# Two attention layers on one core: rotary columns of four heads per weight group, keys in four banks, filter steps moved

## The reference, cut to what matters

```python
h = rmsnorm(x, g_mix[l]);  p = h @ w_in[l]
c_q = rmsnorm(p[..., :384], g_q[l])
q = (c_q @ w_uq[l]).reshape(b, s, 8, 64 + 32)        # 8 heads, 64 plain columns + 32 rotary columns each
q_rope = apply_rope(q[..., 64:], cos, sin)           # t1*cos - t2*sin, t2*cos + t1*sin
c_kv = rmsnorm(p[..., 384:640], g_kv[l])
kv = (c_kv @ w_ukv[l]).reshape(b, s, 8, 64 + 64)     # keys, values
k_rope = apply_rope(p[..., 640:672], cos, sin)       # one for all heads
y_attn = attention(q_nope, q_rope, k_nope, k_rope, v)
a, gt = split(p[..., 672:], 2);  u = a * sigmoid(gt)
u = dwconv(u, w_dw_conv[l], b_dw_conv[l])            # 31 taps over 512 channels
u = silu(layernorm(u, g_conv_ln[l], b_conv_ln[l]))
x = x + concat([y_attn, u]) @ w_o[l]                 # then the feed-forward part
```

## Time and profile before

| | |
|---|---|
| median of three runs | 1910.74 us |
| the profiled execution: its time | 1910.56 us |
| its span, first to last instruction | 1908.8 us |
| TensorE busy, mean granted clock | 96% of the span, 0.982 |
| VectorE, ScalarE busy | 70%, 52% |
| chain that ended last | TensorE 76%, VectorE 11%, no wait shown 6%, ScalarE 6% |

### The profile page before, as it was taken

How to read it: one execution, slowest core, us unless ns; L and a number is a source line. 1 busy time by engine, 2 the same in 40 slices (tenths; PEclk the granted TensorE clock), 3 DMA queues, 4 the chain that set the end, 5 groups by cost and what they waited for, 6 DMA issues and landing times.

```text
span 1908.8 us, 27050 instructions
## 1 busy us (share of the span) xinstructions
PE 1824.7 (96%) x8939; PEld 1451.0 (76%) x8939; DVE 1331.8 (70%) x1873; ACT 986.3 (52%) x1556; POOL 191.7 (10%) x135
## 2 busy tenths in 40 slices
PE   6989999999999998999999999997998999999998
PEld 5765778888888875678888888886655678888887
DVE  6979777777655888967777755695676477777544
ACT  5478654444433478764444433674655554444322
POOL 0100120000133200020000033200012300000111
PEclk9999999999999998999999999998999999999999
DMA  5230233333233330023333233434000223332332
GB/s 168 71 77 1 66 90 98 91 97 96 82 94 111 92 83 12 29 83 100 98 99 99 74 97 94 110 94 133 1 2 1 89 67 98 99 99 82 88 98 75
DMA packets 294697, 154.47 MB, mean 81 GB/s; under 512 B 29621, under 2 KB 292695, under 8 KB 294615
## 3 DMA queue, kind: packets, MB, share of 16 engines
q1 hardware_dynamic: 294196, 153.26, 28.0%
q10 hardware_dynamic: 419, 0.17, 0.0%
HBM read 151.31 MB, written 2.10 MB: 80 GB/s over the span
## 4 chain that ended last, share of the span: by engine, by line
PE 76%; DVE 11%; issue 6%; ACT 6%; DMA 0%; DVEq 0%; SPq 0%; ACTq 0%
PE bank L548 23%; PE bank L550 23%; PE bank L549 23%; DVE cacc L1674 4%; DVE w_lo L1537 2%; PE bank L921 1%; PE bank L961 1%; PE bank L940 1%; DVE nmax L1757 1%; ACT w_hi L1120 1%; DVE pr L2002 1%; PE bank L700 1%; DVE nmax L1986 1%; PE bank L1036 0%; DMA x_in<-in_x 0%
## 5 line engine op out<-in xcount | busy, mean ns | idle before, releaser
L1120 ACT ACTIVATE w_hi<-raw 128x1024 fp32r<-128x1024 f32 (+2 forms) x321 | 333.5, 1041 | 507.2 <-PE bank L550 502.4
L1537 DVE TENSOR_TENSOR w_lo<-raw,w_hi 128x1024 fp32r<-128x1024 f32 (+2 forms) x321 | 401.3, 1251 | 260.6 <-ACT w_hi L1120 259.9
L548 PE MATMUL bank<-h_hi,w_hi 128*128 128x512 f32 x1448 | 570.3, 394 | 10.8 <-DVE w_lo L1537 10.7
L549 PE MATMUL bank<-h_lo,w_hi 128*128 128x512 f32 x1448 | 564.9, 390 | 0.0
L550 PE MATMUL bank<-h_hi,w_lo 128*128 128x512 f32 x1448 | 564.8, 390 | 0.0
L548 PEld LDWEIGHTS bank<-h_hi,w_hi 128*128 128x128 f32 x1448 | 272.7, 188 | 74.8 <-issue 11.7
L549 PEld LDWEIGHTS bank<-h_lo,w_hi 128*128 128x128 f32 x1448 | 272.7, 188 | 58.2 <-issue 2.2
L550 PEld LDWEIGHTS bank<-h_hi,w_lo 128*128 128x128 f32 x1448 | 272.7, 188 | 57.1
L548 PE MATMUL bank<-a_hi,w_hi 128*128 128x512 f32 x528 | 206.1, 390 | 0.0
L550 PE MATMUL bank<-a_hi,w_lo 128*128 128x512 f32 x528 | 205.5, 389 | 0.0
L549 PE MATMUL bank<-a_lo,w_hi 128*128 128x512 f32 x528 | 205.4, 389 | 0.0
(11 more groups left out here) (314 smaller groups left out, 2217.5 us busy)
## 6 DMA issues: line engine op xcount, KB each, us to landing
raw<-in_w_up SPq DMA_DIRECT2D x132, 512.0 KB, 3.7
raw<-in_w_in SPq DMA_DIRECT2D x39, 512.0 KB, 3.9
raw<-in_w_down SPq DMA_DIRECT2D x48, 384.0 KB, 3.1
raw<-in_w_down SPq DMA_DIRECT2D x48, 320.0 KB, 2.9
raw<-in_w_o SPq DMA_DIRECT2D x16, 512.0 KB, 3.5
raw<-in_cmp_w SPq DMA_DIRECT2D x8, 512.0 KB, 4.0
raw<-in_w_out SPq DMA_DIRECT2D x8, 512.0 KB, 4.7
x_in<-in_x SPq DMA_DIRECT2D x4, 512.0 KB, 7.5
```

Of the source, the lines that this page charges most:

```text
L548: mm(o, wh, mh, start=start, stop=False)
L549: mm(o, wh, ml, start=False, stop=False)
L1120: last = A_(dst(w_hi), src(raw), ACT.Copy)
L1537: last = v.tensor_tensor(dst(w_lo), src(raw), dst(w_hi).bitcast(f32), ALU.subtract)
```

## The change

In the first two layers:

- Query slabs 0 and 3 are the wide ones (`UQ_N`); slab 3 carries the rotary columns of heads 4 to 7, into bank 6, and TensorE's wait for the rotary keys goes with it. The four small DMAs of the rotary columns move from slab 2 to slab 3.
- The tables lie in `sq` and `ssq2`, tensors of their own, and are copied at input slabs 2 to 5, two copies each.
- The keys use banks 4, 2, 0, 3, each once; their waits are for query copies (`qn_done`), and values and scores wait for the key copies instead.
- VectorE: all four cosine products of the second group stand together, behind the value slab's low part; 18 filter steps are issued around the query and key slabs where there were 10, and 3 at each step of attention where there were 4.

```diff
-        tabs = at("tabs", [P, 2, SEQ], 0)
...
-        UQ_B, K_B, V_B = ((0, 1), (2,), (3, 6), (5,)), (4, 2), (0, 1, 3, 6)
+        UQ_B, K_B, V_B = ((0, 1), (2,), (3,), (5, 6)), (4, 2, 0, 3), (0, 1, 3, 6)
+        UQ_N = (2, 1, 1, 2)
...
-                    if j == 2:
+                    if j == 3:
                         pe.wait_ge(kr_done.sem, kr_done.at(L, 1))
...
-                    if i == 1:
-                        pe.wait_ge(qn_done.sem, qn_done.at(L, 4))
-                    elif i > 1:
-                        pe.wait_ge(k_done.sem, k_done.at(L, 2 * (i - 1)))
+                    if i >= 1:
+                        pe.wait_ge(qn_done.sem, qn_done.at(L, (0, 4, 4, 6)[i]))
...
-                        pe.wait_ge(k_done.sem, k_done.at(L, H - 2))
+                        pe.wait_ge(k_done.sem, k_done.at(L, 2))
...
+                    if t % 2 == 0:
+                        pe.wait_ge(k_done.sem, k_done.at(L, 6 + t))
...
-                    if i >= 12:
-                        for q in (2 * i - 24, 2 * i - 23):
-                            for z in range(2):
-                                A_(tabs[q * ROPE:(q + 1) * ROPE, z, :], trig[z * ROPE:(z + 1) * ROPE, :], ACT.Copy).then_inc(tab_done.sem, 1)
+                    if 2 <= i < 6:
+                        q = slice((i - 2) * ROPE, (i - 1) * ROPE)
+                        A_(sq[q, :], trig[0:ROPE, :], ACT.Copy).then_inc(tab_done.sem, 1)
+                        A_(ssq2[q, :], trig[ROPE:2 * ROPE, :], ACT.Copy).then_inc(tab_done.sem, 1)
...
-                dve.wait_ge(slab_used.sem, g * RAW + (S_UQ + 3))
+                split(g, S_UQ + 2 + SPL)
+                conv(2)
+                dve.wait_ge(slab_used.sem, g * RAW + (S_UQ + 4))
                 sine_part(1)
-                split(g, S_UQ + 2 + SPL)
-                cosine_part(1, 0, 2)
                 split(g, S_UQ + 3 + SPL)
-                cosine_part(1, 2, 4)
+                cosine_part(1, 0, 4)
+                conv(8)
                 conv(6)
-                conv(3)
                 split(g, S_UKV + SPL)
-                conv(1)
+                conv(2)
...
-                    conv(4)
+                    conv(3)
```

More of the change, by code:

```diff
@@ L436, in split_aps @@
             if S_UQ <= n0 < S_UKV:
-                used = lambda w: w[:, n0 % w.shape[1], 0:KQ * P * (2 - (n0 - S_UQ) % 2)]
+                used = lambda w: w[:, n0 % w.shape[1], 0:KQ * P * UQ_N[n0 - S_UQ]]
                 return [(used, used)]
@@ L483, in _ @@
                 for j in range(H // 2):
-                    n = P * (2 - j % 2)
+                    n = P * UQ_N[j]
                     to = slot(S_UQ + j, KQ, n)
@@ L492, in _ @@
                             sp.dma_start(dst, src).then_inc(uq_ready[j], 16)
-                    if j % 2 == 0:
+                    if UQ_N[j] == 2:
                         for q in range(4):
-                            sp.dma_start(to[:, :, P + q * ROPE:P + (q + 1) * ROPE], of[:, :, 2 * j + q, NOPE:HQ]).then_inc(uq_ready[j], 16)
+                            sp.dma_start(to[:, :, P + q * ROPE:P + (q + 1) * ROPE], of[:, :, j // 2 * 4 + q, NOPE:HQ]).then_inc(uq_ready[j], 16)
                 for z in range(2):
@@ L660, in _ @@
                         pe.wait_ge(u_done.sem, u_done.at(L, KC))
-                    w = parts(S_UQ + j, KQ, P * (2 - j % 2))
-                    for z in range(2 - j % 2):
+                    w = parts(S_UQ + j, KQ, P * UQ_N[j])
+                    for z in range(UQ_N[j]):
                         for k in range(KQ):
@@ L673, in _ @@
                 for i in range(H // 2):
-                    if i == 1:
-                        pe.wait_ge(qn_done.sem, qn_done.at(L, 4))
-                    elif i > 1:
-                        pe.wait_ge(k_done.sem, k_done.at(L, 2 * (i - 1)))
+                    if i >= 1:
+                        pe.wait_ge(qn_done.sem, qn_done.at(L, (0, 4, 4, 6)[i]))
                     for k in range(KKV):
-                        last = mm3(bank[K_B[i % 2]][:, :], [z[:, k, i * P:(i + 1) * P] for z in w],
+                        last = mm3(bank[K_B[i]][:, :], [z[:, k, i * P:(i + 1) * P] for z in w],
                                    (c_hi[:, KQ + k, :], c_lo[:, KQ + k, :]), k == 0, k == KKV - 1)
@@ L1113, in split @@
                     j = n0 - S_UQ
-                    act.wait_ge(uq_ready[j], (L + 1) * 16 * (1 + 4 * (1 - j % 2)))
+                    act.wait_ge(uq_ready[j], (L + 1) * 16 * (1 + 4 * (UQ_N[j] - 1)))
                 if not isinstance(g, int) and S_UKV <= n0 < S_O:
@@ L1262, in _ @@
                     for e in range(2):
-                        A_(kT[0:NOPE, 2 * i + e, :], bank[K_B[i % 2]][e * NOPE:(e + 1) * NOPE, :],
+                        A_(kT[0:NOPE, 2 * i + e, :], bank[K_B[i]][e * NOPE:(e + 1) * NOPE, :],
                            ACT.Copy).then_inc(k_done.sem, 1)
@@ L1719, in sine_part @@
                 def sine_part(z):
-                    v.scalar_tensor_tensor(qs[:, z, :], bank[UQ_B[2 * z][1]][:, :], SCALE1, tabs[:, 1, :], ALU.mult, ALU.mult)\
+                    v.scalar_tensor_tensor(qs[:, z, :], bank[UQ_B[3 * z][1]][:, :], SCALE1, ssq2[:, :], ALU.mult, ALU.mult)\
                         .then_inc(qs_done.sem, 1)
@@ L1725, in cosine_part @@
                         r = slice(q * ROPE, (q + 1) * ROPE)
-                        v.scalar_tensor_tensor(qT[64:96, 4 * z + q, :], bank[UQ_B[2 * z][1]][r, :], SCALE1, tabs[r, 0, :],
+                        v.scalar_tensor_tensor(qT[64:96, 4 * z + q, :], bank[UQ_B[3 * z][1]][r, :], SCALE1, sq[r, :],
                                                ALU.mult, ALU.mult).then_inc(qr_done.sem, 1)
```

## The result

| | before | after |
|---|---|---|
| median | 1909.65 us (1907.61 to 1913.0, 5 runs) | 1918.92 us (1917.78 to 1919.41, 5 runs) |
| profiled execution: time, span | 1910.56, 1908.8 | 1919.41, 1917.6 |
| mean granted clock | 0.982 | 0.980 |

The change is slower by 9.3 us: ratio 1.0045, 95% interval 1.003 to 1.0059. The prediction was 1909.7 us, range 1904.0 to 1915.5; the time lies outside, on the side of rival B.

A forecast was written before the change was run, and what follows sets the result against it. TensorE, busy 96% of the span, was taken to bound the kernel, with VectorE arriving almost together at the sums. A gain of 0.5 us per layer, 1.0 in all, from the median of 1910.74 gave 1909.7 us, range 1904.0 to 1915.5.

The forecast's parts named there:

- rival B: Ahead of the sums: low clock behind TensorE's new wait, 1.7 to 3.3 us per layer, time 1914.7; chance 0.23.
- The tables cost nothing: Table copies moved to input slabs 2 to 5: cost 0 there, gain 0.5 us on ScalarE.
- front of slabs: Ahead of the keys: table and wide-slab moves together start the keys at 120.9 us and not at 121.40.
- C: Filter's end: VectorE isn't late, so unit 15's 3.3 us count in full, 6.6 in all, 1904.1; chance 0.25.
- D: Whole change does nothing, since unit 0's scores still need ScalarE's queue: 1910.7 us; chance 0.06.
- forecast A: Front's gain ends in TensorE's wait for the filter: 1908 to 1911.5 us; chance 0.46.
- Attention: Unit 6 to unit 15: TensorE leads, 1.6 us gained, plus 1.7 ahead of that; unit 15's scores 3.3 earlier.
- The end of the filter: Unit 15's maxima to the sums: VectorE has 14 steps left, TensorE waits 3.3 us; gain 0.5 us per layer.
- I took 0.3 us for it: Filter steps behind unit 1's maxima: extra cost of running beside POOL's first sum, taken as 0.3 us.
- The bound of 0.9: Filter steps beside POOL's sum: nearest row allows 0.9 us extra; in full, gain 0 per layer and 1910.7.

The follow-up runs named there:

- before again: The kernel before, unedited, profiled once more beside the unedited change: 1908.23 us.
- two shifted kernels: The kernel before with 17, and in a second kernel 8, overwritten matmuls added at the start of the third layer: 1913.21 and 1908.92 us.
- The filled wait: The changed kernel with 16 overwritten matmuls in TensorE's wait ahead of the sums: 1912.49 us, ratio 1.0017 to before.
- second batch: Both kernels, unedited, measured and profiled once more: before 1908.23 us, change 1919.12 us, ratio 1.0057.

## Why the prediction was wrong

**What held.** The place of each event in layer 1 held. The profiled execution of the change comes to that layer 0.73 us earlier than before's (first query slab at 105.03 against 105.76), so 0.73 is added to its times here. The key wait is gone. TensorE waits 2.06 us ahead of unit 0's scores (2 predicted) and 3.03 ahead of unit 2's (3.5). The first maximum is at 139.4 (139.5). From unit 6 on attention goes at TensorE's pace, 3.81 us a step, and unit 15's scores are at 194.7 (194.1). The low part of `yq` comes 1.41 us late (1.5), and TensorE waits 3.83 ahead of the sums (3.3). The tables cost nothing, and the front of slabs gained 0.45. Rivals C and D fell, and the forecast A too.

**The step that failed first is the base of the sum**, in "Attention": "Ahead of that the wait at 157.66 and the low clock behind it go or shrink: 1.7." The wait behaves as said, but that low clock was an event of one execution. Three others of the same code in these layers (before again, and the two shifted kernels) do without it, and their layers take 124.6 to 125.4 us where the rows had 127.4. The prediction set beside the median (1910.74) only that execution's total (1910.56), and the total hid it: that execution was long in the layers and short in the third layer (654.8, against 656.9 to 658.2 in the three others). The predicted 0.5 us gained per layer was against 127.4. The others are 2.0 to 2.1 us shorter in the first layer (1.8 of it between unit 0's and unit 15's scores) and 2.7 to 2.8 in the second, where the key wait was also shorter, 3.0 instead of 4.6. A gain of 0.5 per layer counted against the rows is none against them: the base was 4.9 us too long in the two layers.

**The second is the low clock behind the new wait**, which stood there as rival B at 0.23. It fell in both layers, in both profiled executions of the change, 3.4 us at the low level each time. From the first sum to the first matmul on `uq` the change takes 22.72 us and before 21.03 (212.12 to 233.15): 1.7 more in the first layer, and 2.0 in the second. The filled wait shows how much of this is the clock: it gave back 1.3 and 1.6. The other 0.4 per layer is the second sum's wait for its own low part, a term that the prediction did not have. B's price was 2.5 per layer, so the clock cost less than that; the rest of the miss is in the two other steps.

**The third is the size of the gain in "The end of the filter": "Gain 0.5 us per layer".** The first sum starts at 212.5 on before's time base, 0.4 us later than before's and not 0.5 earlier: 0.9 per layer. Most of it is "I took 0.3 us for it", the cost of POOL's first sum beside filter steps. The four steps behind unit 1's maxima took 3.75 us beside that sum, one of them 1.64 us where each alone takes some 0.7. In the kernel with ten steps in the front POOL's sum comes later (148.49), and the same four took 2.73:

```profile
138.53 2.73 DVE L1674 SCALAR_TENSOR_TENSOR cacc<-u_pad,lc,cacc 128x512 f32<-128x512 f32 x4
```

That is 1.0 us, and it stays on the path: from the first maximum to unit 15's scores the change takes 55.31 us (138.69 to 194.00) and that kernel 54.31 (134.35 to 188.66). Six steps beside POOL's second sum took 5.33 us, and six alone 4.06 there: 1.3. Before paid for that one too: its four steps at 200.46 took 3.86, 1.1 more than 2.73. The bound of 0.9 that the prediction named was itself read a little low from that row. So 0.7 of the 0.9 is POOL's first sum (1.0 less the 0.3 that was taken) and 0.2 its second. Before, POOL's first sum (153.23 to 154.94) lay for most of its length beside two maxima, which took what they take alone:

```profile
153.73 1.28 DVE L1757 TENSOR_REDUCE nmax<-bank 128x1 f32<-128x512 f32 x2
```

The Trainium skill ("SBUF — State Buffer", section "Who interferes with whom") states that a VectorE instruction with two SBUF inputs contends with a GpSimd instruction that reads SBUF, and that a reduction does not. The traces agree with both halves: 3.75 us against 2.73 for the four filter steps, 1.28 against 1.29 for the two maxima.

In the first layer that makes -0.5 + 0.9 + 1.7 = +2.1 us, as the profiles have it, and with the 2.0 behind the sums +2.4 in the second. With the 4.9 of the base it is 9.4 us, the difference of the layers. That this equals the measured 9.3 is in part luck: the second batch measured 10.8, and the third layer adds 1.0 to 4.4 by which profile of before it is set against.

**What stays open**: why the change's third layer was at 659 us in both of its profiles, where before's was at 654.8 and 658.2.

And one thing that the prediction didn't ask: it took the filter's new places for given with the banks. The idle time in the front that eight steps "fill" was also the lead that the banks gained for the first maximum. The banks with the old places are worth 5 to 7 us.

## What to carry to other kernels

When a wait is removed on the bound engine, ask which engine sets the next event, and leave the gained lead to it: work moved into another engine's gaps delays everything queued behind it, and the same work taken out of later gaps leaves them empty. Here either move made the two layers 12 to 15 us longer, and both together 13. Where two placements are changed at once, price them one by one; here one part was worth -5 us and the other +12. Profile a kernel twice before building a sum on a low-clock stretch in it: what stands in one execution need not in the next, and a total that agrees with the median doesn't prove that its parts do.

## What the runs showed of the hardware

- Behind the same wait of TensorE (1.73 us for `pt`, in the same kernel) the clock fell to the low level (granted share 0.5) in one execution and stayed at full in another. Behind 3.83 us it fell in all six cases seen: four in the change, two with its filter steps alone.
- 16 matmuls without use, in a wait of 3.8 us, made a layer 1.3 to 1.6 us shorter, and the kernel some 6 us.
- Four filter steps on VectorE took 2.73 us, and 3.75 with POOL's sum of 128x512 beside them (3.74 or 3.75 in the first layer of all four kernels where they met, the change in both of its profiles). Two maxima from PSUM beside the same sum took 1.28 us, as they do alone.
- In 13 executions one unchanged stretch took 654.5 to 659.6 us, following its time at the low level at some 0.4 us per us.
